# Weight tiles of a long one-core kernel begin 32 bytes further on with every pair of chunks, and the loops over chunks are written out

## The reference

```python
def conv_gated_ffn(xn, w_gate, w_up, dw_w, dw_b, w_down):          # gate_up (1024 -> 2 x 2816)
    g = causal_depthwise_conv(xn @ w_gate, dw_w, dw_b)
    return (jax.nn.gelu(g, approximate=True) * (xn @ w_up)) @ w_down

def _sq_relu_mlp(h, w1, w2):                                       # ffn_up0/1 and ffn_down0/1
    return jnp.square(jax.nn.relu(h @ w1)) @ w2                    # 1024 -> 4096 -> 1024

for layer in range(DEPTH_2):
    mix = _even_mixer(...) if layer % 2 == 0 else _retention(...)
    h = _layer_norm(DEEPNORM_ALPHA * h + mix, ...)
    h = _layer_norm(DEEPNORM_ALPHA * h + _sq_relu_mlp(h, w1[layer], w2[layer]), ...)
return h[:, N_META:, :]
```

## The kernel before, in words

| operand | before | after |
|---|---|---|
| whi, wlo, five long stages | 128 and 0 in turn | both slots 128 + 32j for pair j = 0..7 (128, 160, 192, 224, 0, 32, 64, 96) |
| whi, wlo, other stages | 128 and 0 in turn | 128 and 0 in turn (`kv`: 128 instead of 0) |
| pw (`ple`), gw (`ple_gate`), fw (`gate_up`, first chunk) | 64, 64, 96 | 128 |
| moving, 256 and 258 columns | 64 | 64 |
| moving, `ffn_up0` and four of `ret_qk` (274 columns) | 0 | 0 |
| moving, `ffn_down0` (272) | 0, 64, 128, 192 in turn with k | 64 |
| moving, `even_dqk`, `even_v`, `even_fqk`, `even_out` (272) | 0 | 64 |
| moving, `ret_v` (272) | 0 | 0 |

## Time and profile before

### The profile page before, as it was taken

One profiled execution on the slowest core, in us unless ns is written; L12 is line 12 of the kernel. 1 busy time (PEld: TensorE's weight loads), 2 busy tenths in 40 slices (PEclk: granted clock), 3 DMA queues, 4 the chain that ended last, 5 costly groups with the idle time before them and its releaser, 6 DMA issues.

```text
span 1116.8 us, 24238 instructions
## 1 busy us (share of the span) xinstructions
PE 1091.4 (98%) x8961; PEld 1056.4 (95%) x8961; DVE 780.7 (70%) x1403; ACT 621.1 (56%) x1192; POOL 358.2 (32%) x396
## 2 busy tenths in 40 slices
PE   9998999999989999999999999999999999999996
PEld 8976999999989999899999999999989999999996
DVE  5776588887478777767887554795556567987554
ACT  5657566556455657765656334563336646665433
POOL 2102323334302412245666111300034335675120
PEclk9999999999999999999999999999999999999998
DMA  8463447775556623225555545654414565556550
GB/s 240 127 190 114 115 118 211 195 191 164 192 173 196 219 76 114 77 93 172 180 159 187 182 159 185 212 186 154 150 39 152 187 202 175 179 181 204 189 187 38
DMA packets 202938, 180.63 MB, mean 162 GB/s; under 512 B 6864, under 2 KB 200819, under 8 KB 202739
## 3 DMA queue, kind: packets, MB, share of 16 engines
q1 hardware_dynamic: 202179, 175.74, 50.7%
q0 software_dynamic: 688, 3.94, 0.9%
HBM read 176.28 MB, written 1.05 MB: 159 GB/s over the span
## 4 chain that ended last, share of the span: by engine, by line
PE 88%; DVE 5%; ACT 3%; issue 2%; POOL 1%; DMA 1%; SPq 0%; ACTq 0%; DVEq 0%; POOLq 0%
PE ps L1979 26%; PE ps L1980 26%; PE ps L1981 26%; DVE wlo L1342 2%; PE ps L2406 1%; PE ps L2150 1%; PE ps L2536 1%; ACT whi L797 1%; POOL acc L602 1%; PE ps L2514 1%; PE ps L2389 1%; DMA raw<-w_ple_gate 1%; PE ps L2185 1%; PE ps L2364 1%; PE ps L2484 0%
## 5 line engine op out<-in xcount | busy, mean ns | idle before, releaser
L1342 DVE TENSOR_TENSOR wlo<-raw,whi 128x1024 fp32r<-128x1024 f32 x316 | 396.5, 1291 | 152.2 <-ACT whi L797 150.4
L797 ACT ACTIVATE whi<-raw 128x1024 fp32r<-128x1024 f32 x315 | 317.5, 1051 | 157.8 <-PE ps L1981 145.7
L1979 PE MATMUL ps<-xh,whi 128*128 128x256 f32 (+1 forms) x880 | 250.0, 284 | 0.7 <-DVE wlo L1342 0.4
L1980 PE MATMUL ps<-xl,whi 128*128 128x256 f32 (+1 forms) x880 | 247.4, 281 | 0.0
L1981 PE MATMUL ps<-xh,wlo 128*128 128x256 f32 (+1 forms) x880 | 247.3, 281 | 0.0
L1979 PE MATMUL ps<-xrh,whi 128*128 128x274 f32 (+2 forms) x832 | 241.2, 290 | 0.0
L1980 PE MATMUL ps<-xrl,whi 128*128 128x274 f32 (+2 forms) x832 | 238.4, 287 | 0.0
L1981 PE MATMUL ps<-xrh,wlo 128*128 128x274 f32 (+2 forms) x832 | 238.4, 287 | 0.0
L1981 PE MATMUL ps<-fh,wlo 128*128 128x256 f32 (+1 forms) x688 | 193.3, 281 | 0.0
L1980 PE MATMUL ps<-fl,whi 128*128 128x256 f32 (+1 forms) x688 | 193.1, 281 | 0.0
L1979 PE MATMUL ps<-fh,whi 128*128 128x256 f32 (+1 forms) x688 | 193.1, 281 | 0.0
(11 more groups left out here) (371 smaller groups left out, 1618.6 us busy)
## 6 DMA issues: line engine op xcount, KB each, us to landing
raw<-ffn_w SPq DMA_DIRECT2D x128, 512.0 KB, 4.4
raw<-ret_w_in SPq DMA_DIRECT2D x48, 512.0 KB, 4.4
raw<-even_w_in SPq DMA_DIRECT2D x24, 512.0 KB, 4.7
raw<-w_ffn_gate SPq DMA_DIRECT2D x22, 512.0 KB, 4.0
raw<-w_ffn_up SPq DMA_DIRECT2D x22, 512.0 KB, 5.2
raw<-w_ffn_down SPq DMA_DIRECT2D x16, 512.0 KB, 4.4
raw<-ret_w_out SPq DMA_DIRECT2D x16, 512.0 KB, 4.1
raw<-w_in SPq DMA_DIRECT2D x11, 512.0 KB, 5.2
```

The source lines that it names most:

```text
L797: A(whi[:, slot, s * 1024:s * 1024 + 1024], raw[:, slot, s * 1024:s * 1024 + 1024], ACT.Copy).then_inc(w_hi_ready, 1)
L1342: V.tensor_tensor(wlo[:, slot, s * 1024:s * 1024 + 1024], raw[:, slot, s * 1024:s * 1024 + 1024], f32(whi[:, slot, s * 1024:s * 1024 + 102 ...
L1979: T.matmul(dst, w[0], x[0], start=first, stop=False)
L1980: T.matmul(dst, w[0], x[1], start=False, stop=False)
```

## The change

1. The tiles of `whi` and `wlo` begin `line_step(c)` elements into their slot, on every engine that writes or reads them. In the five long stages that is 8 elements (32 bytes) more with each pair of chunks; elsewhere the old 128 bytes for the odd slot. A slot is 32 columns longer (`WS = CH + 64`), so that both begin at place 128.
2. The side tiles `pw`, `gw` and `fw` are moved to place 128, and the moving operands of the even layer and of `ffn_down0` to place 64 (new views `xoh`, `xeh`, `f0h`, with rows of 320 columns).
3. Every loop over chunks is written out, on all engines. What each engine computes, its waits and the order of its instructions stay.

```diff
-XS, WS = 320, CH + 32
+XS, WS = 320, CH + 64
...
-    with eng.Fori(apart, turns) as i:
+    for i in range(apart, turns):
         body(i)
...
+def line_step(c):
+
+    for name, count in (("ffn_up0", 16), ("ffn_down0", 16), ("ffn_up1", 16), ("ffn_down1", 16), ("gate_up", 16)):
+        if C0[name] <= c < C0[name] + count:
+            return 8 * ((c - C0[name]) // 2)
+    return 0 if c == C0["kv"] else 32 * (c % 2)
...
+        xoh, xol = xh_mem[:, :, META:META + N2], xl_mem[:, :, META:META + N2]
...
-        pw_at = m1.at
+        pw_at = m1.at + 64
...
-        kt_at = m1.at
+        m1.at = kt_at = line_at(m1.at, 128)
...
-        diag_at = m1.at
+        m1.at = diag_at = line_at(m1.at, 128)
...
+        f0h, f0l = (nc.alloc_sbuf_tensor_at(name, [P, FT2, XS], F32R, offset=f0_at + 4 * n * FT2 * XS)[:, :, 0:N2]
+                    for n, name in enumerate(("f0h", "f0l")))
...
-        gw_hi, gw_lo = (nc.alloc_sbuf_tensor_at(name, [P, CH], F32R, offset=arena0 + at0 + 4 * (META + FT * N1))
+        gw_hi, gw_lo = (nc.alloc_sbuf_tensor_at(name, [P, CH], F32R, offset=arena0 + at0 + 4 * (2 * META + FT * N1))
...
+        xeh, xel = (x[:, :, META:META + N2] for x in xr_mem)
...
-                    A(whi[:, slot, s * 1024:s * 1024 + 1024], raw[:, slot, s * 1024:s * 1024 + 1024], ACT.Copy).then_inc(w_hi_ready, 1)
+                    w0 = line_step(2 * use + slot) + s * 1024
+                    A(whi[:, slot, w0:w0 + 1024], raw[:, slot, s * 1024:s * 1024 + 1024], ACT.Copy).then_inc(w_hi_ready, 1)
...
-            def tile(slot, at0, n):
+            def tile(c, at0, n):
+
+                slot, at0 = c % 2, at0 + line_step(c)
                 return whi[:, slot, at0:at0 + n], wlo[:, slot, at0:at0 + n]
...
-                with pe.Fori(0, 2) as i:
+                for i in range(0, 2):
...
-            with pe.Fori(2, FT // 2) as i:
+            for i in range(2, FT // 2):
```

More of the change, by code:

```diff
@@ L231, in __call__, with line_at @@
                 return t
-        def line_at(byte):
-            return byte + (64 - byte) % 256
+        def line_at(byte, start=64):
+            return byte + (start - byte) % 256
         m1 = Arena()
@@ L810, in split_rope_at @@
                 slot = c % 2
-                to = whi[:, slot, 0:n * (width + ROPE)].rearrange("p (k n) -> p k n", k=n)
+                w0 = line_step(c)
+                to = whi[:, slot, w0:w0 + n * (width + ROPE)].rearrange("p (k n) -> p k n", k=n)
                 src = raw[:, slot, 0:n * width].rearrange("p (k n) -> p k n", k=n)
@@ L1254, in _ @@
             residual(S_LN, "even_out", 1, 0, ALL)
-            ffn_up("ffn_up0", FT, 0, ALL, fh)
+            ffn_up("ffn_up0", FT, 0, ALL, f0h)
             residual(S_LN + 1, "ffn_down0", 4, 1, ALL)
@@ L1341, in split_lo @@
                     dve.wait_ge(w_hi_ready, 2 * c + s + 1)
-                    V.tensor_tensor(wlo[:, slot, s * 1024:s * 1024 + 1024], raw[:, slot, s * 1024:s * 1024 + 1024],
-                                    f32(whi[:, slot, s * 1024:s * 1024 + 1024]), ALU.subtract).then_inc(w_lo_ready, 1)
+                    w0 = line_step(c) + s * 1024
+                    V.tensor_tensor(wlo[:, slot, w0:w0 + 1024], raw[:, slot, s * 1024:s * 1024 + 1024],
+                                    f32(whi[:, slot, w0:w0 + 1024]), ALU.subtract).then_inc(w_lo_ready, 1)
             def split_at(c, halves=(0, 1)):
@@ L1362, in split_rope_at @@
                 slot = c % 2
-                lo, hi = (w[:, slot, 0:n * (width + ROPE)].rearrange("p (k n) -> p k n", k=n) for w in (wlo, whi))
+                w0 = line_step(c)
+                lo, hi = (w[:, slot, w0:w0 + n * (width + ROPE)].rearrange("p (k n) -> p k n", k=n) for w in (wlo, whi))
                 src = raw[:, slot, 0:n * width].rearrange("p (k n) -> p k n", k=n)
@@ L1997, in product @@
                     for dst, col, m in outs:
-                        ins = three(dst, tile(slot, k * cols + col, m), [v[:, k0 + k, at_x] for v in x],
+                        ins = three(dst, tile(c, k * cols + col, m), [v[:, k0 + k, at_x] for v in x],
                                     first and n == 0, last and n == kt - 1)
@@ L2164, in _ @@
                     for dst, col, _ in outs:
-                        ins = three(dst, tile(c % 2, D * k + 2 * P * j + col, P), [v[:, 3 + k, TOK1] for v in rows_q], k == 0, k == 1)
+                        ins = three(dst, tile(c, D * k + 2 * P * j + col, P), [v[:, 3 + k, TOK1] for v in rows_q], k == 0, k == 1)
                 ins.then_inc(mm_done, 1)
@@ L2170, in _ @@
                 for k in range(2):
-                    wv = tile(c % 2, D * k + HEADS * NOPE, HEADS * VDIM)
+                    wv = tile(c, D * k + HEADS * NOPE, HEADS * VDIM)
                     xv = [v[:, 3 + k, P * t:P * t + P] for v in rows_q]
@@ L2266, in _, with slot_tile @@
                     stat(S_MIX)
-            def slot_tile(slot):
-                return lambda at0: tile(slot, at0, P)
+            def slot_tile(c):
+                return lambda at0: tile(c, at0, P)
             def two_chunks(name, weights, ready, free, beside=None):
@@ L2327, in _ @@
             c = C0["ple_gate"]
-            two_chunks("ple_gate", (lambda at0: (gw_hi[:, at0:at0 + P], gw_lo[:, at0:at0 + P]), slot_tile((c + 1) % 2)),
+            two_chunks("ple_gate", (lambda at0: (gw_hi[:, at0:at0 + P], gw_lo[:, at0:at0 + P]), slot_tile(c + 1)),
                        x_from(X_PLE), lambda u: None)
@@ L2332, in _ @@
                 product(c + j, (c + j) % 2, pair("ple_gate", j, N1), rows_x1, TOK1, 256).then_inc(mm_done, 1)
-            outputs("even_dqk", 2, ALL, rows_r, x_from(X_B), qk_ready, lambda j: 2 * j + 2)
+            outputs("even_dqk", 2, ALL, rows_e, x_from(X_B), qk_ready, lambda j: 2 * j + 2)
             def qkv_products(c, slot, b, x):
@@ L2341, in qkv_products @@
                     for m in range(2):
-                        yield three(ps[b + m][:, 0:N2], tile(slot, 256 * k + P * m, P), [v[:, k, ALL] for v in x], k == 0, k == KD - 1)
+                        yield three(ps[b + m][:, 0:N2], tile(c, 256 * k + P * m, P), [v[:, k, ALL] for v in x], k == 0, k == KD - 1)
             pe.wait_ge(gates_in, 32)
@@ L2434, in _ @@
                 steps = 2 * KD
-                for n, ins in enumerate(qkv_products(chunk, chunk % 2, 2 * (c % 2), rows_r)):
+                for n, ins in enumerate(qkv_products(chunk, chunk % 2, 2 * (c % 2), rows_e)):
                     if n + 1 == steps:
@@ L2454, in _ @@
                 wait(pe, tile_ready, TILES[S_LN] + 2 * (j - 1) if j >= 2 else 0)
-                product(C0["even_out"] + j, (C0["even_out"] + j) % 2, pair("even_out", j, N2), rows_x, ALL, 256,
+                product(C0["even_out"] + j, (C0["even_out"] + j) % 2, pair("even_out", j, N2), rows_o, ALL, 256,
                         ready=even_mix if j == 0 else None).then_inc(mm_done, 1)
```

46 lines of the change are left out of this document (25 added, 21 removed).

## The result

The changed kernel takes 1126.12 us (median of 3 runs, 1126.01 to 1127.03) against 1119.04 us: 1.0065 times the time of before, 95% interval 1.0051 to 1.0079, so 7.1 us slower. Forecast were 1122.9 us and a range to 1127.5. Its profiled execution took 1126.01 us with a span of 1123.8 us and a mean granted clock of 0.992; that is 7.0 us more span than before.

The account below looks back on a forecast made before the run. It took the spacing of TensorE's matmuls to bound the kernel. The terms 4.6 + 0.4 + 0.6 - 0.6 + 0 - 0.7 - 0.4 + 0 gave +3.9 us, so 1122.9 us, with a range of 1115.5 to 1127.5.

Parts of the forecast that it names:

- The distance counts: Matmul spacing depends on the distance between weight and moving places, by 1 to 7 ns; 64 and 192 both 113.3 ns.
- Sweep at 256 columns: `gate_up` and `ffn_down1`: 1152 matmuls leave places 128 and 0, +4.6 us; bounds -2.5 and +7.7 us.
- Rhythm: Coming back from a bad place leaves the 256-column stream slow for about a chunk, twice: +0.4 us.
- 258 columns: Sweep in `ffn_up1`: 576 matmuls at +1 ns, +0.6 us; bounds -6.5 and +3.9 us.
- 274 columns: Sweep in `ffn_up0`: places 64 and 192 save 1.7 ns, odd ones half, -0.6 us; bounds +2.5 and -6 us.
- `ffn_down0`: 768 matmuls pass from four distances in turn to all eight: 0 us, bounds +2 and -4 us.
- Even layer: 768 matmuls go from distances 128 and 0 to 64 and 192, 125.9 to 125.0 ns: -0.7 us.
- Side tiles: `pw`, `gw` and `fw`, 144 matmuls, go to place 128: -0.4 us, bounds -1.0 and 0.
- Loops: Written-out loops save nothing on TensorE and the longer program does not come late: 0 us.
- Rival 1: Places do not matter; 120 against 113.3 ns is history, the slow rhythm: 1119.0 us, chance 0.15.
- Rival 2: Odd 32-byte places (32, 96, 160, 224) are free of the stall, so faster: 1112.2 us, chance 0.20.
- Rival 3: Each change of place is a new start, so 256-column streams never settle: 1129 us, chance 0.15.

Follow-up runs that it names:

- E5: E2 with the moving tiles x1 and f1 at place 128 instead of 64, weights still at 128 and 0: 1131.71 us, 1.011 of the kernel before.
- E6: E5 with the weights of `gate_up`, `down` and `ffn_down1` also 64 bytes further on, at 192 and 64: 1121.13 us, 1.0018 of the kernel before.
- E2: The changed kernel without its sweep, weights at 128 and 0 in turn in the five stages: 1117.79 us, 0.9991 of the kernel before.
- E1: The kernel before with its loops over chunks written out and nothing else: 1119.38 us against 1119.0, ratio 1.0002.
- E9: E8 with the 256-column stages at place 128 in both slots, no alternation there: 1120.34 us, 1.0015 of the kernel before.
- E11: E9 with only chunks 8 and 14 of `gate_up` at place 0: 1117.31 us, 0.9996 of the kernel before.
- E10: E7 with the first four chunks of each of the five stages at place 128: 1121.18 us, 1.0026 of the kernel before.
- E7: The changed kernel with both slots at place 0 in all five stages, no sweep: 1126.21 us, 1.0066 of the kernel before.
- E8: The changed kernel without its sweep, cheapest weight place per width in wider stages, alternation kept at 256 columns: 1113.97 us, 0.9955 of the kernel before.

## Why the prediction was right in direction and short in size

- *What bounds the kernel*: right. TensorE's idle time grew by 0.6 us only, and the stage table holds 6.8 of the 7.0 us.
- *The distance counts, 64 and 192 alike at 256 columns*: right, and now shown by E5 and E6 rather than read from side tiles.
- *Sweep at 256 columns*, +4.6 us: the term that was mis-sized. The two stages lost 3.9 + 3.8 = 7.7 us, of which about 6.4 is the price of the six other places. Places 64 and 192 cost 6.6 and 5.3 ns over 113.3 (I took 6.7 for both, 2.6 us; measured 2.3). Places 96 and 224 cost 5.0 and 6.7 ns; I had halved the one row that said 4.7, in case it was only the slow rhythm: 0.9 us forecast, 2.2 measured. Places 32 and 160 cost 4.6 and 6.7 ns in `ffn_down1` where I took 3: 1.1 forecast, 1.9 measured with the 4.1 ns that 160 cost in `gate_up`. The bound of all six at 120.0 was the nearer one.
- *Rhythm*, +0.4: short by about 0.8 us. Place 0 never came back in either stage (2 x 96 x 4.4 ns = 0.8 us), and `gate_up` stayed slow for three chunks behind the sweep (0.6 us), as its first step from 0 to 128 did not take; 0.2 us of slow rhythm at its chunk 2 were there before. I had expected the stream to settle by itself within a chunk; between interruptions it did so only at such a step, and the sweep has few.
- *258 columns*, +0.6: measured +0.3. *274 columns*, -0.6: measured +0.6, the wrong sign. I had carried the 1.7 ns of the earlier trace rows (272 columns) to 274, where a distance of 64 or 192 saves nothing (126.7 ns) and places 96 and 160 cost 2.2 and 1.0.
- *`ffn_down0`*, 0: measured -0.1. *Even layer*, -0.7: measured -0.6. Both came out by luck of an average: the earlier trace rows seemed to give 125.0 ns at distances 64 and 192 alike, where its steps of 0.01 us over six matmuls are 1.7 ns each; E2's trace has 123.4 ns at 64 and 126.6 at 192, and the eight places of `ffn_down0` after range from 123.4 to 126.7. *Side tiles*, -0.4: not to be told from the scatter of the stages with many waits. *Loops*, 0: E1 says 0.4 us at a ratio of 1.0002.
- Rival 1 (places do not matter, 1119.0) falls with E2, E5 and E6. The Trainium skill's rule behind it ("TensorE: Matmul & The Clock Gate", Step-by-step: what each phase is for; separate read ports for moving operand and weights) does not describe these streams: in E5 only the moving operand moved by 64 bytes, and 256 columns went from 113.3 to 119.2 ns.
- Rival 2 (odd 32-byte places are free, 1112.2) falls at once: 117.7 to 120.0 ns there in `ffn_down1`.
- Rival 3 (the slow rhythm stays, 1129) was half right. Its reason, each change of place is a new start, is wrong: between 128 and 0 a change of place left the fast rhythm alone 363 times in 364, and the step from 0 to 128 ended the slow one. Its symptom, place 0 at 117.8 ns, was there.
- The other rule of the Trainium skill, that a taken branch stalls for its fetch ("Runtime: NRT & Kernel Launch", Instruction fetch mechanics), is for a target outside the two-page window. E1, without the branches, was not faster (1.0002); whether the targets lay inside the window or the stalls were hidden, no run shows.

Open: why a distance of 64 is fast and others are not. That the two reads meet in the same part of the memory in turn would fit, but no run shows the memory itself. Open too is what makes 15 of 52 steps fail, and E9's and E11's spread over 6 to 9 us, which would fit stages that by chance enter in one rhythm or the other and keep it; only one execution of each was profiled.

## What to carry to other kernels

Where back-to-back matmuls with small tiles set the time, look at the address of weights and moving operand modulo 256 together: here the good distance was worth 6 ns of 120, for no work at all, and the best choice depended on the number of columns, so measure each width rather than sweep. At 256 columns keep what changes the place from chunk to chunk, since a constant place, even the best, can stay in the slow rhythm for a whole stage. And when one row of a trace may be either a steady cost or history, price it at both: here it was a steady cost, and halving it left out 0.9 of the 3.2 us by which the forecast was short.

## What the runs showed of the hardware that was not expected

- A stream of 256-column matmuls has two stable spacings at the same places, 113.3 and 117.8 ns, and keeps the one it is in while nothing interrupts it: 117.8 ns for the chunks of `gate_up` in E9, 113.3 for those of `ffn_down1`. 274 columns have 126.7 and 130.1 ns (E10 and E7).
- The way out is one-sided: weights stepping from place 0 to 128 ended the slow one 37 times in 52, from 128 to 0 never in 9. In E6, with both operands moved by 64, a step from 64 to 192 ended it.
- Behind an interruption the place has a say as well: slow in 64 of 72 cases at place 0, in 26 of 105 at place 128.
- At 272 columns, moving operand at 64, the weights at 128 give 123.3 ns (E8), at 0 126.6 (two chunks of `ffn_down0` after): distances 64 and 192 are not alike there, as they are at 256 columns.
